# Forgetting attention with its decay rows as bf16 pieces, heads in pairs on array halves, sample outputs gathered on VectorE, and cache pages between half slots

## The reference

```python
logf = log_sigmoid(n @ w_f + b_f)
F = cumsum(concat(past_logf, logf), axis=1)
s = einsum('bqhd,bkhd->bhqk', q, k) * 64 ** -0.5
s = s + Fq[..., :, None] - Fk[..., None, :]
s = where(k_pos <= q_pos, s, -1e30)
p = softmax(s)
o = einsum('bhqk,bkhd->bqhd', p, v)
x = x + g1 * (o @ w_o)
```

## Time and profile before

| what | us |
|---|---|
| median of 3 runs (1397.68 to 1407.69) | 1401.73 |
| the profiled execution | 1397.8 |
| its span, first to last instruction | 1396.0 |
| key stage, 786 to 910 | 124 |
| value loop, first value product to first product of the output projection | 117.1 |

### The profile page before, as it was taken

The page is one execution under the profiler, slowest core; times in us unless marked ns, Lnnn a source line. Parts: engine busy times, 40 slices in busy tenths (PEclk is TensorE's granted clock), DMA queues, the critical chain, the costliest instruction groups (busy, mean ns, idle before and its releaser), DMA issues.

```text
span 1396.0 us, 19882 instructions
## 1 busy us (share of the span) xinstructions
PE 1267.1 (91%) x7082; PEld 734.2 (53%) x7094; DVE 471.8 (34%) x1455; ACT 218.8 (16%) x442; POOL 137.5 (10%) x262
## 2 busy tenths in 40 slices
PE   6999886799998999999999978899999889999995
PEld 4786653478785443344346756644466443344333
DVE  1233434341014444445443100032322634445434
ACT  2001223422002210000002100032211210000001
POOL 3330111110001000000000122212210000000000
PEclk8999997899999899999999988977799799999998
DMA  9945755575749399999998699967755579999991
GB/s 368 379 156 212 252 184 207 215 256 183 301 149 411 146 380 415 400 404 408 398 408 333 249 356 385 368 235 248 276 208 225 198 276 404 391 412 402 408 408 69
DMA packets 74352, 421.73 MB, mean 302 GB/s; under 512 B 9224, under 2 KB 10520, under 8 KB 35744
## 3 DMA queue, kind: packets, MB, share of 16 engines
q1 hardware_dynamic: 43488, 314.04, 56.8%
q0 software_dynamic: 29728, 101.20, 19.9%
q10 hardware_dynamic: 1056, 5.36, 1.0%
HBM read 398.43 MB, written 22.14 MB: 301 GB/s over the span
## 4 chain that ended last, share of the span: by engine, by line
PE 76%; DMA 8%; DVE 7%; issue 4%; ACT 2%; DVEq 1%; POOL 1%; POOLq 1%; SPq 0%; ACTq 0%
PE bank L735 74%; DMA ring<-wstream 6%; DMA arena<-kcache 2%; DVE arena L1962 1%; PE bank L778 1%; DVE x L1978 1%; PE bank L1265 1%; DVEq L1957 1%; ACT arena L1497 1%; ACT xn L1380 1%; POOL arena L667 1%; DVE arena L1991 1%; DVE arena L1670 1%; POOLq L664 0%; DMA x<-x_in 0%
## 5 line engine op out<-in xcount | busy, mean ns | idle before, releaser
L735 PE MATMUL bank<-arena 128*32 128x256 f32 (+9 forms) x2048 | 348.0, 459 | 61.7 <-DVE x L1978 20.9
L735 PE MATMUL bank<-ring,arena 128*64 128x512 f32 (+2 forms) x1856 | 382.1, 560 | 12.9 <-issue 5.8
L735 PEld LDWEIGHTS bank<-arena 128*32 128x32 f32 (+5 forms) x2048 | 178.1, 150 | 210.4 <-issue 138.6
L735 PEld LDWEIGHTS bank<-ring,arena 128*64 128x64 f32 (+2 forms) x1856 | 138.5, 138 | 237.4 <-issue 209.7
L1362 ACT ACTIVATE arena<-bank 128x256 f32<-128x256 f32 (+4 forms) x187 | 87.8, 473 | 607.0 <-PE bank L735 516.7
L735 PE MATMUL bank<-h,ring 128*128 128x264 f32 x640 | 145.2, 387 | 0.6 <-DMA ring<-wstream 0.6
L735 PEld LDWEIGHTS bank<-h,ring 128*128 128x128 f32 x640 | 120.9, 190 | 22.3 <-issue 1.9
L735 PE MATMUL bank<-arena,ring 128*128 128x264 f32 x512 | 117.5, 392 | 2.5 <-DMA ring<-wstream 1.9
L1978 DVE SCALAR_TENSOR_TENSOR x<-bank,mod,x 128x256 f32<-128x256 f32 x256 | 119.3, 481 | 0.0
L735 PEld LDWEIGHTS bank<-arena,ring 128*128 128x128 f32 x512 | 98.6, 194 | 20.4 <-issue 2.7
L667 POOL DMA_DIRECT2D arena<-kcache x64 | 33.9, 530 | 541.4 <-PE bank L735 407.7
(11 more groups left out here) (232 smaller groups left out, 779.2 us busy)
## 6 DMA issues: line engine op xcount, KB each, us to landing
ring<-wstream SPq DMA_DIRECT2D x296, 1024.0 KB, 8.5
arena<-kcache POOLq DMA_DIRECT2D x64, 512.0 KB, 8.0
arena<-vcache POOLq DMA_DIRECT2D x64, 512.0 KB, 5.0
arena<-state POOLq DMA_DIRECT2D x28, 512.0 KB, 4.5
ss_out<-arena POOLq DMA_DIRECT2D x28, 512.0 KB, 3.8
xn<-state POOLq DMA_DIRECT2D x4, 512.0 KB, 5.2
ss_out<-xn POOLq DMA_DIRECT2D x4, 512.0 KB, 6.1
sp_out<-arena ACTq DMA_DIRECT2D x4, 512.0 KB, 2.7
```

The source lines that it names most:

```text
L735: ins = nc.tensor.matmul(out, w, rhs, start=start, stop=stop, skip_group_check=True)
```

## The change

In the key stage the eight pages before a slot are split: four pages, half a slot, four pages, half a slot. In the value loop the two heads of a turn are issued alternately on the two halves of the array's rows (scores) or columns (values). The decay row is written by VectorE as a sum of three bf16 pieces on 3 x 16 of each half's 64 partitions, and its product runs in bf16 over 64 rows. The pages go in runs of four, two and two. The samples' own token and the turning leave the loop: VectorE scales each turn's result with a weight that is zero except on the rows of sample b and adds it up, and after the loop it folds the heads together, adds the own token (whose values ScalarE's queue has laid out in rows by four small copies) and one product turns everything at once. POOL's hardware loop over the 56 value pages becomes straight code.

```diff
@@ plan_turns
-    t.add("ownT", X1)
     t.add("oT", X2)
     for b in range(NS):
         t.add(("pv", b), (X0, M)[b % 2])
         for hh in range(2):
             t.add(("pT", hh, b), L[2 + hh])
-        for hh in range(2):
-            t.add(("po", hh, b), L[hh])
+        t.add(("po", b), L[0])
         if b + 1 < NS:
             head_scores(b + 1)
@@ POOL
-            with pool.Fori(0, NPAGES // PAGES - 1) as lap:
+            for b in range(1, NS):
                 for r in range(PAGES):
-                    page_id = page_of(lap * PAGES + (NPAGES + PAGES + r))
-                    pool.wait_ge(page_used, lap * PAGES + (NPAGES // 2 + r + 1))
+                    page_id = page_of(NPAGES + NPG * b + r)
+                    if r < NPG - 1:
+                        pool.wait_ge(page_used, NPAGES // 2 + (NPG - 1) * (b - 1) + r + 1)
+                    else:
+                        result(pool, ("pv", b - 1))
                     load_page(vcache, r, page_id)
@@ TensorE, key stage
             for i in range(8):
-                for n in range(4 * i, 4 * i + 4):
-                    key_pages(n)
-                take_slot(S_KV + i)
-                if i < 4:
-                    for m in range(2):
+                for m in range(2):
+                    for n in range(4 * i + 2 * m, 4 * i + 2 * m + 2):
+                        key_pages(n)
+                    if m == 0:
+                        take_slot(S_KV + i)
+                    if i < 4:
                         columns(("fk", i, m), S_KV + i, m, n2)
-                else:
-                    values("fv", S_KV + i, n2, i - 4)
+                    else:
+                        values("fv", S_KV + i, n2, i - 4, m)
...
-                    mm(ps[0:FH, 0:TP], lf_tok[:, 0, :], c_("upto"), True, False)
-                    mm(ps[0:FH, P:TP], lf_tok[:, 1, :], c_("upto")[:, 0:P], False, True, full)
+                    mm(ps[:, 0:TP], lf_rep[:, 0, :], c_("upto"), True, False)
+                    mm(ps[:, P:TP], lf_rep[:, 1, :], c_("upto")[:, 0:P], False, True, full)
@@ TensorE, value loop
-            def head_scores(b, hh):
-                rows = slice(64 * hh, 64 * hh + 64)
-                ps, full = begin(("ps", hh, b))
-                only = bc(c_("negeye", FH)[:, 2 * b + hh:2 * b + hh + 1], [FH, P])
+            def head_scores(b):
+                halves = [begin(("ps", hh, b)) for hh in range(2)]
                 for c in range(2):
                     cols = slice(0, P) if c == 0 else slice(P, 3 * P)
                     keys = slice(0, (c + 1) * P)
-                    mm(ps[:, cols], fq[rows, b, c * P:(c + 1) * P], fk[rows, b, keys], True, False)
-                    mm(ps[:, cols], only, Fsb[:, keys], False, True, full if c else None)
+                    for hh, (ps, full) in enumerate(halves):
+                        rows = slice(64 * hh, 64 * hh + 64)
+                        mm(ps[:, cols], fq[rows, b, c * P:(c + 1) * P], fk[rows, b, keys], True, False)
+                    for hh, (ps, full) in enumerate(halves):
+                        rows = slice(64 * hh, 64 * hh + 64)
+                        only = bc(only_bf[rows, 2 * b + hh:2 * b + hh + 1], [64, P])
+                        mm(ps[:, cols], only, F_piece[rows, 3, keys], False, True, full if c else None)
...
-            def head_values(b, hh):
-                moved(pe, ("pT", hh, b))
-                ps, full = begin(("po", hh, b))
...
+            def head_values(b):
+                for hh in range(2):
+                    moved(pe, ("pT", hh, b))
+                ps, full = begin(("po", b))
+                for c in range(2):
+                    for hh in range(2):
...
+                        mm(ps[rows, cols], fv[:, c, feats], pT_sb[:, hh, of], c == 0, c == 1,
+                           full if c and hh else None)
...
             for b in range(NS):
-                value_page(b, 0)
...
+                for g in range(4):
+                    value_page(b, g)
                 head_turn(b, 0)
...
                 head_turn(b, 1)
...
                 value_page(b, 4)
...
                 value_page(b, 5)
+                head_values(b)
                 if b + 1 < NS:
-                    head_scores(b + 1, 0)
+                    head_scores(b + 1)
                 value_page(b, 6)
...
                 value_page(b, 7)
-                own_value(b)
-                if b:
-                    sample_turn(b - 1)
-            sample_turn(NS - 1)
+            pe.wait_ge(o_rows_ready, 1)
+            ps, full = begin("oT")
+            mm(ps[:, 0:P], o_rows.rearrange("p u d -> p (u d)"), ident, True, True, full)
@@ ScalarE
+            for s in range(MG):
+                act.dma_start(v_rows[MW * s:MW * s + MW, :], v_sam[:, 256 * s:256 * s + 256]).then_inc(rows_in, 16)
...
-                for hh in range(2):
-                    rows = slice(64 * hh, 64 * hh + 64)
-                    ps = result(act, ("po", hh, b))
-                    copy(fo[rows, b, 0:TP], ps[rows, 0:TP]).then_inc(free(("po", hh, b)), 1)
+                ps = result(act, ("po", b))
+                copy(fo[:, b, 0:TP], ps[:, 0:TP]).then_inc(free(("po", b)), 1)
@@ VectorE
+            step(nc.vector.tensor_copy(F_piece[:, 0, :], ps[:, 0:TP]))
+            wait()
+            tt(F_rest[:, 0, :], ps[:, 0:TP], F_piece[:, 0, :], ALU.subtract).then_inc(free("F"), 1)
...
             def sample_out(b):
                 ps = result(dve, ("pv", b))
-                tsc(o_sam[:, b, :], ps[:, 0:256], dinv, None, ALU.mult).then_inc(free(("pv", b)), 1)
+                wait()
+                flat_o = o_all.rearrange("p h d -> p (h d)")
+                if b:
+                    ins = stt(flat_o, ps[:, 0:256], weight8[:, b:b + 1], flat_o, ALU.mult, ALU.add)
...
             sample_out(NS - 1)
+            step(tt(o_head, o_all, bc(c_("of_head").unsqueeze(2), [P, 4, HD]), ALU.mult))
+            wait()
+            step(nc.vector.tensor_reduce(o_sum, o_head.rearrange("p h d -> p d h"), AX, ALU.add))
+            dve.wait_ge(rows_in, 16 * MG)
+            wait()
+            stt(o_rows, bc(v_rows.unsqueeze(1), [P, 2, HD]), own_w, bc(o_sum.unsqueeze(1), [P, 2, HD]), ALU.mult,
+                ALU.add).then_inc(o_rows_ready, 1)
```

More of the change, by code:

```diff
@@ L466, in build @@
         fz = fx.take(4, T, rows=FH)
-        lf_tok = fx.take(2, FH)
-        Fsb = fx.take(TP, rows=FH)
+        lf_rep = fx.take(2, P)
+        F_piece = fx.take(4 * (TP // 2)).bitcast(BF16).rearrange("p (v n) -> p v n", v=4)
+        only_bf = fx.take(FH // 2).bitcast(BF16)
         lf_diag = fx.take(P, rows=FH)
@@ L482, in build @@
         dinv = fx.take(1)
-        own_p = fx.take(NS)
-        own_pT = fx.take(P, rows=NS)
+        v_rows = fx.take(HD)
+        weight8 = fx.take(NS)
+        own_w = fx.take(1)
+        o_all = fx.take(4, HD)
+        o_head = fx.take(4, HD)
+        o_sum = fx.take(HD)
+        o_rows = fx.take(2, HD)
         pages = Region(arena_cols - PAGES * D)
@@ L814, in samples_in, with values @@
                     mm(ps[rows, 0:256], src[:, k, :], w[:, k, :], k < MG, k >= KT - MG, full if k == KT - 1 else None)
-            def values(key, n, src, i):
+            def values(key, n, src, i, c):
                 w = slot(n)
-                for c in range(2):
-                    ps, full = begin((key, i, c))
-                    for k in range(KT):
-                        mm(ps[:, 0:256], src[:, k, c * P:(c + 1) * P], w[:, k, :], k == 0, k == KT - 1,
-                           full if k == KT - 1 else None)
+                ps, full = begin((key, i, c))
+                for k in range(KT):
+                    mm(ps[:, 0:256], src[:, k, c * P:(c + 1) * P], w[:, k, :], k == 0, k == KT - 1,
+                       full if k == KT - 1 else None)
             for i in range(8):
@@ L1283, in value_page @@
                     mm(ps[strip(s), 0:256], pT_past[:, g, strip(s)], page[:, m % PAGES, 256 * s:256 * s + 256],
-                       g == 0, False, page_used if s == MG - 1 else None)
-            def own_value(b):
-                ps, full = bank[at["pv", b][0]], filled[at["pv", b][0]]
-                for s in range(MG):
-                    mm(ps[strip(s), 0:256], own_pT[:, strip(s)], v_sam[:, 256 * s:256 * s + 256], False, True,
-                       full if s == MG - 1 else None)
-            def sample_turn(b):
-                if b == 0:
-                    begin("oT")
-                moved(pe, ("pv", b))
-                ps, full = bank[at["oT"][0]], filled[at["oT"][0]]
-                for c in range(2):
-                    picks = ident.rearrange("p (s n) -> p s n", s=MG)[:, :, 4 * b + 2 * c:4 * b + 2 * c + 2]
-                    at_col = (2 * b + c) * NS
-                    mm(ps[:, at_col:at_col + NS], o_sam[:, b, c * P:(c + 1) * P], picks, True, True,
-                       full if b == NS - 1 and c else None)
+                       g == 0, g == NPG - 1, None if s < MG - 1 else page_used if g < NPG - 1 else filled[at["pv", b][0]])
```

(15 more changed lines are left out.)

70 lines of the change are left out of this document (40 added, 30 removed).

## The result

Four runs of the changed kernel have a median of 1359.96 us (1355.84 to 1364.73), the four of the kernel before on the same chip 1403.69 us. The forecast was 1360, range 1346 to 1386. The ratio compares only runs in the same state of the chip, so it is not exactly the quotient of the two medians.

The account below looks back on a forecast made before the run. It took DMA and TensorE to share the key stage's bound and TensorE to bound the value loop; 1397.8 - 9 (key stage) - 2 (junction) - 31 (loop) = 1355.8, plus 3.9 to the median, so 1360 us, range 1346 to 1386.

Parts of the forecast that it names:

- What binds the loop afterwards: Value loop: page transfers, not TensorE, are late next, at 1.275 us per page and 10.6 per turn; loop 86, gain 31.
- Key stage and junction: Half slots fill later transfer holes, gaining 9 us (bounds -2 to 12); earlier maxima shorten the junction by 2 (0 to 3).
- The wait for bank 0: Value loop, each turn: scores reuse the bank values filled, so TensorE waits 0.6 us for ScalarE to move it out.
- Scores: Value loop: both heads' float32 products cost one head's, about half of 2.07 us; with bf16 decay rows 1.55 per turn.
- The clock: Value loop: TensorE at full clock 63% of the time, as before; its turn 9.3 us, between 7.8 full and 14.0 half.
- The four copies on ScalarE's queue: Junction: small copies of 2.1 us if each costs a POOL issue's 0.53, covered by the longer maxima on VectorE.
- The end: After the last turn: VectorE's four instructions, one turning product and four copies take 3.2 us to the projection, against 2.54 before.
- That the halves do not work side by side: Rival, value loop: array halves take turns, 13.4 us per turn, loop 106, median 1380; chance 0.12.
- Slower pages: Rival, value loop: pages arrive at 333 GB/s, 1.57 us each, loop 98, median 1372; chance 0.10.
- A key stage without gain: Rival, key stage: transfers and TensorE still wait for each other at half slots, no gain, median 1369; chance 0.10.
- a low clock: Rival, value loop: more page waits keep TensorE's clock low, 14.0 us per turn, loop 115, median 1389; chance 0.05.
- a low clock with single file: Rival, value loop: halves take turns at low clock, 20 us per turn, loop 163, median 1437, slower than before; chance 0.03.

## Why the prediction was right, step by step

*What binds the loop afterwards* held. Transfers were forecast to be late next, at 1.275 us per page and 10.6 us per turn; pages arrive 1.29 apart, and the loops last 87.7 and 85.4 us (86 forecast). The sum behind the longer one: the forecast's bound of 81 us for 56 pages with start and end, some 4 us in the two dips, and 2.5 us more at start and end, where for one the first issue comes 1.8 us after the loop's start and not 0.9. Of the signs named, one did not come: the DMA share of the whole loop is 0.89 and not above 0.95, though it is 1.03 on the plateau.

*Key stage and junction* held in size: 9 and 2 forecast, 7 to 10 and 1.7 measured. *The wait for bank 0* was put at 0.6 and measured about 0.5. *Values* of both heads were put at 0.80, side by side, and start side by side.

*Scores* held in their reason and were mis-sized: 1.55 forecast, 1.07 measured. The halves do work side by side, and the float32 products of both heads cost those of one, as the forecast has it (1.51 for both and for one). What it had wrong is the price of one head. It took the 2.07 of the earlier trace rows for the price of the products; 0.56 of it comes with the 16-row products between 64-row ones, and goes when the rows are equal, a part of the edit that I passed over as the vessel of the bf16 pieces. Step by step in the runs: 4.14 for two heads before, about 3.0 (two times 1.51) for two heads with equal rows, one apart from the other, 1.51 in pairs, 1.07 with bf16.

*The clock* was carried over from before, 63% of the time at full speed. It rose: 0.78 to 0.91 with pages and 0.98 without. The edit of the rows alone brings it to 0.98 in the kernel before with PE busy for 96% of the loop, so it was these products that cost the clock and not the load on TensorE. The two errors, together with 1.5 us for the softmax chain that I had not priced, left TensorE's own turn at 8.7 where 9.3 was forecast. Either lies under the transfers' 10.2, so they did not reach the sum. That much is luck, and so is the median within 0.1 us of 1360: the four runs lie 9 us apart.

*Small terms.* The four copies on ScalarE's queue were bounded at 2.1 and called covered; with the store they ran for 4.2 us (905.88 to 910.09) and put ScalarE's copy behind VectorE's end. The end was put at 3.2; from the last page's start to the projection it is 4.0 (994.62 to 998.64), which with a page's 0.57 leaves 3.45:

```profile
994.62 0.64 PE L745 MATMUL bank<-arena 128*32 128x256 f32 x8 [0.51 <-DMA arena<-vcache]
...
997.46 0.49 PE L745 MATMUL bank<-cst,arena 128*128 128x128 f32 x2 [2.20 <-DVE arena L2181]
...
998.64 0.81 PE L745 MATMUL bank<-arena,ring 128*128 128x264 f32 x1 [0.69 <-DVE arena L2187]
```

*The rivals.* That the halves do not work side by side, priced at a loop of 106, falls with the starts of the pairs and with the 1.51; issuing the heads in single file (loop 85.5) is no trial of it, since they overlap there too. Slower pages (333 GB/s) fall with the plateau near 410. A key stage without gain, a low clock, and a low clock with single file fall with the stages above.

The Trainium skill's figure of about 358 GB/s (DMA: Bandwidth & Descriptors, Specifications) is worked out there as half of what two cores share. This trace, with one core at work, does not agree with it in the changed kernel either: 403 to 412 GB/s in the first plateau.

## What to carry to other kernels

When short products alternate, look at their shapes before their number: products over 16 rows between products over 64 rows put both kinds about twice as far apart, kept the other half of the array from working beside them, and went with a lower granted clock while TensorE was busy throughout. Filling the rows with zeros, a dozen lines in the kernel before, was worth 26 us here. When TensorE is busy all the time at a clock of 0.8, that clock is itself something to explain, not a constant to carry into the sum. An experiment that changes the order of issue does not show what side by side is worth until the starts of the products say that the overlap is gone. And run the changed stage without its transfers once: it tells at one look how far TensorE's gain can reach before the pages stop it.

## What was not expected of the hardware

*Clock without gaps.* In the loop before without pages PE is busy for 113.7 of 114.4 us at a granted clock of 0.80; with 64 rows for the decay product and nothing else changed PE is busy for 87.5 of 90.8 us, with pages, and the clock is 0.98.

*Order of issue.* With 64 rows and single file the second head's products, issued behind all of the first head's, start before the first head's last one (936.44 against 937.08). Order of issue and order of starts differ between the halves of the array.

*POOL's pause.* All eight profiles with value pages have a pause of POOL of 3.2 to 3.5 us before the 42nd of the 56 issues: 3.22 at 969.79 above, 3.46 in the kernel before, there in a hardware loop. The page that had to be used first had been used well before (its last product starts at 964.58). The second dip of the transfers, some 2 us, follows it. Its cause is open; no run here was aimed at it.

*Small copies.* The four copies of the samples' new values kept ScalarE's queue for 0.73 to 1.38 us each, where an issue of a whole page takes POOL 0.53.
